# First attention of a three-block kernel: GpSimd takes over the probability multiplies of row tiles 1 to 3

## The chip, the cores and the metric

The kernel runs on one core of a Trainium2 chip. It is one program on five engines with separate instruction queues: TensorE (PE; its weight loads are listed as PEld), VectorE (DVE), ScalarE (ACT), GpSimd (POOL) and SyncE (SP), which wait for each other on semaphores. The metric is the device time of one execution in microseconds.

## The reference, cut to what matters

The whole computation is a transformer block with sparse and sliding-window attention on 512 tokens, followed by two more mixer blocks. The change is in the attention of the first block. For each of 16 heads (two groups of four for each kind of attention) and each query row:

```python
# kind 1: selected blocks (all causal keys here), kind 0: compressed + windowed keys
s = q @ k.T * scale - slope * dist            # NEG_INF where masked
p = softmax(s)                                # exp(s - max) / sum
o = gc[..., 0:1] * o_c + gc[..., 1:2] * o_s + gc[..., 2:3] * o_w   # gates per row and head
# sliding window of 128 with a sink
m = max(max(s), sink);  e = exp(s - m)
prob = e / (sum(e) + exp(sink - m));  o = prob @ v
```

Because a gate is one number per row and head, the kernel multiplies the exponentials by reciprocal sum and gate before the product with the values.

## The kernel before, in words

The attention of the first block works on "quads": four heads of one group g (0 or 1), one row tile t (0 to 3, 128 query rows each) and one kind. Quad number n is 6t + 2·kind + g, so there are 24. In kinds 0 and 1 the scores are 128·(t+1) keys wide (kind 0 also has a compressed part of 32 columns, finished earlier); kind 2, the sliding window, is 128 wide for t = 0 and 256 wide after that. Each quad goes through five steps:

1. TensorE computes the scores of each head into one of four PSUM banks (`pe_slot_scores`, L902 and L903). A "slot" is one bank's worth: two heads at width 256, one at 384 and 512. A slot waits for the exponentials of the slot four before it (`b_exped`).
2. VectorE adds the distances and takes the row minimum (`dve_slot_least`, L2552).
3. ScalarE exponentiates into the SBUF tile `p1` and sums the rows into `st1` (`act_slot_exp`, L1754).
4. VectorE takes the reciprocals of the sums (L2570) and multiplies each head's probabilities in place, four instructions per quad (`dve_quad_scale`: L2579 by reciprocal and gate, L2577 by the reciprocal alone for kind 2). The last one raises `b_scaled`.
5. TensorE waits for `b_scaled`, transposes the quad 128 columns at a time (`pe_quad_turn`, L924; the compressed part, L920, doesn't wait), ScalarE copies the result out of PSUM (L1768), and TensorE multiplies by the values (L948, L945). ScalarE and VectorE then split the output into two parts (L1796, L2593).

The order of the work is written out by hand. On TensorE, `pe_quads` issues for each quad its transposes chunk by chunk, and behind each chunk up to two score slots of later quads, then pairs of value products. On VectorE, `dve_quads` issues for each quad n the minima of the slots that lie four slots ahead, then the multiplies of quad n+1, then outputs that are ready:

```python
    for q in qs:
        for slot in slots_behind(qs, q.n):
            dve_slot_least(k, dve, qs, slot)
        if q.n + 1 < len(qs):
            dve_quad_scale(k, dve, qs, qs[q.n + 1])
```

ScalarE's order is: copy of chunk i of the transposes, then exponentials of the two slots whose scores were issued behind chunk i-1.

GpSimd's work in the whole program is to split the weights, as SyncE loads them, into a high and a low part (L497, L499). Before the attention it splits the output projection's weights; the next ones, of the feed-forward layer (`w_first_hi`), wait for the last attention output (`o_lo`).

Of the kernel before, what the change touches and what calls it, by code (L numbers as in the profile page):

```python
# [9 lines left out]
ALU = mybir.AluOpType  # L10
# [13 lines left out]
GROUPS, PER_G = 2, 4  # L24
# [15 lines left out]
SLOTS_P = 8  # L40
# [22 lines left out]
class Signal:  # L63
# [37 lines left out]

    "gcol gates_ps gates_th gates blocks k_hi k_lo v_copied q_hi q_lo cmp_ps hid_sq hid_a hid_th hid ck_ps ck_hi ck_lo "
    "zeroed sink_neg cmp_scored cmp_least cmp_exped cmp_ready "
    "b_scored b_least b_aux b_exped b_sunk b_scaled b_turned b_pt b_valued o_hi o_lo "

    "scored least exped normed turned pt valued gated "

# [25 lines left out]
class Kernel:  # L133
    def __init__(self, nc, ins, outs, known):
        self.nc, self.ins, self.outs = nc, ins, outs
        self.sig = {n: Signal(nc, n, known) for n in SIGNALS}
        self.x_dram = nc.dram_tensor("x_scratch", [P, TX, D], F32).ap()
        self.gate_dram = nc.dram_tensor("gate_scratch", [3, D], F32).ap()
        self.lay_memory()
        self.list_weights()  # L140
        self.bank_order = bank_order()
        self.ahead = iter(OUT0_AHEAD)
        self.turn8_read = {4: ("turn_tmp", ("h8", TA - 1, 1)), 7: None}
        self.at_before = [None, None]
        sp_program(self, nc.sync)
        pool_program(self, nc.gpsimd)
        pe_program(self, nc.tensor)
        act_program(self, nc.scalar)
        dve_program(self, nc.vector)
# [269 lines left out]
def product_behind(tile):  # L419

    what = tile[0]
    if what == "kv":
        return ("kv", 0, 3) if tile[1] == 0 else ("v", TX - 1)
    if what in ("q", "ff"):
        return (*tile, 3)
    if what in ("o", "gate", "out1"):
        return (what, TX - 1, tile[1])
    if what == "out0":
        return (what, TA - 1, tile[1])
    if what == "down":  # L430
        return (*tile, TX - 1)
    if what == "head":
        return ("z", tile[1], 1)
    if what == "q8":
        return ("row8", 2 * tile[1] + 1, TX - 1)
    return ("kv8", TX + 1) if what == "kv8" else ("z8", 4 * tile[1] + 3)
# [6 lines left out]
def pool_zero_keys(k, pool):  # L443

    s = k.sig
    pool.memset(k.small[:, 3:4], 0.0).then_inc(*s["pool_step"].up())
    pool.wait_ge(*s["pool_step"].now())
    zero = k.small[:, 3:4].rearrange("p (a n) -> p a n", a=1)
    for g in range(GROUPS):
        pool.tensor_copy(k.klo[HD:P, g, 0:2, :], zero[HD:P].to_broadcast([HD, 2, S])).then_inc(*s["pool_step"].up())  # L450
        pool.wait_ge(*s["pool_step"].now())
        pool.tensor_copy(k.klo[0:HD, g, 2:3, :], zero[0:HD].to_broadcast([HD, 1, S])).then_inc(*s["pool_step"].up("k_zero"))
        pool.wait_ge(*s["pool_step"].now())


def pool_program(k, pool):
    s = k.sig
    pool.memset(k.ones[:, :], 1.0).then_inc(*s["ones_set"].up("ones"))
    pool.wait_ge(*s["rms"].at(("x1", 1)))
    for t in range(2, TX):  # L460
        pool.tensor_scalar(k.rows1[:, t, :], k.rows1[:, t, :], k.stat[:, 1, t:t + 1], None, ALU.mult).then_inc(*s["scaled"].up(("x1", t)))
    pair = 0
    for i, (tile, pieces, row0, chunks) in enumerate(k.weights):
        if i == 2:
            pool_zero_keys(k, pool)
        width = max(c0 + n for c0, n, _ in pieces)
        for q in range(0, chunks, 2):
            r = pair % 2
            raw = k.w_raw[:, r, :, 0:width]
            hi, lo = (x[:, q:q + 2, 0:width] for x in k.place(tile))  # L470
            pool.wait_ge(*s[f"w_loaded{r}"].at(pair))
            if q == 0:
                if tile == ("ff", 0):

                    pool.wait_ge(*s["o_lo"].at((TX - 1, 2)))
                elif tile == ("kv8",):

                    pool.wait_ge(*s["y_lo"].at(7))
                elif k.before_in_slot[tile] is not None:
                    pool.wait_ge(*s["prod"].at(product_behind(k.before_in_slot[tile])))  # L480

                if tile == ("ff", 1):
                    pool.wait_ge(*s["rms"].at(("y1", "x", TX - 1)))
                if tile == ("gate", 1):
                    pool.wait_ge(*s["y_added"].at(TX - 1))
                if tile == ("head", 1):
                    pool.wait_ge(*s["rms"].at(("x4", TX - 1)))
                if tile == ("q8", 0):
                    pool.wait_ge(*s["rms"].at(("y3", "x", TA - 1)))
                if tile == ("z8", 0):  # L490
                    pool.wait_ge(*s["rms"].at(("q8", 0)))
            if tile == BY_SCALAR:
                pool.wait_ge(*s["act_step"].at(("w_hi", q)))

            for e in range(2):
                if tile != BY_SCALAR:
                    pool.tensor_scalar(hi[:, e, :], raw[:, e, :], 1.0, 0.0, ALU.mult, ALU.add).then_inc(*s["pool_step"].up())  # L497
                    pool.wait_ge(*s["pool_step"].now())
                m = pool.tensor_tensor(lo[:, e, :], raw[:, e, :], hi[:, e, :], ALU.subtract)  # L499
            m.then_inc(*s["w_split"].up(pair))  # L500
            if q == 0:
                s["w_split"].seen[tile] = s["w_split"].n
            pair += 1
# [73 lines left out]
def quads():  # L577

    out, first = [], 0
    for t in range(TX):  # L580
        for kind in range(3):
            for g in range(GROUPS):
                out.append(Quad(len(out), g, t, kind, first))
                first = out[-1].slots[-1] + 1
    return out
# [12 lines left out]
def turn_number(qs, n, i):  # L598
    return sum(len(q.chunks) for q in qs[:n]) + i


VALUES_AT_ONCE = 2


def value_steps(qs):

    steps, held, step = {}, [], 0
    for q in qs:
        for i in range(len(q.chunks)):
            if len(held) >= VALUES_AT_ONCE:  # L610
                steps[step], held = held[:VALUES_AT_ONCE], held[VALUES_AT_ONCE:]
            if q.g == 1:
# [294 lines left out]
def pe_quad_turn(k, pe, qs, q, i):  # L907

    s, n = k.sig, turn_number(qs, q.n, i)
    what, c = q.chunks[i]  # L910
    if i == 0 and what == "cmp":
        pe.wait_ge(*s["cmp_ready"].at(q.g))
    if what == "keys":
        pe.wait_ge(*s["b_scaled"].at(q.n))
    if n >= 2:
        pe.wait_ge(*s["b_pt"].at(n - 2))
    for e in range(PER_G):
        if what == "cmp":
            x = k.pc[:, q.g, (q.t * PER_G + e) * CMP_W:(q.t * PER_G + e + 1) * CMP_W]
            m = pe.transpose(k.ps[0:CMP_W, 4 + n % 2, e * P:(e + 1) * P], x, k.ident[:, :])  # L920
        else:
            slot, c0 = q.place(e)
            c0 += (c - q.k0) * P
            m = pe.transpose(k.ps[:, 4 + n % 2, e * P:(e + 1) * P], k.p1[:, slot % SLOTS_P, c0:c0 + P], k.ident[:, :])  # L924
    m.then_inc(*s["b_turned"].up((q.n, i)))
# [1633 lines left out]
def dve_quad_scale(k, dve, qs, q):  # L2559

    s, step = k.sig, k.sig["dve_step"]
    f = k.st1[:, q.n % 8, :, :]
    dve.wait_ge(*s["b_exped"].at(q.slots[-1]))
    total = f[:, 1, :]
    if q.kind == 2:
        dve.wait_ge(*s["b_sunk"].at(q.n))
        dve.tensor_tensor(f[:, 2, :], f[:, 1, :], f[:, 3, :], ALU.add).then_inc(*step.up())
        dve.wait_ge(*step.now())
        total = f[:, 2, :]
    dve.reciprocal(f[:, 3, :], total).then_inc(*step.up())  # L2570
    dve.wait_ge(*step.now())
    for e in range(PER_G):
        slot, c0 = q.place(e)
        p = k.p1[:, slot % SLOTS_P, c0:c0 + q.w]
        c = (q.g * PER_G + e) * 3 + 1 + q.kind
        if q.kind == 2:
            m = dve.tensor_scalar(p, p, f[:, 3, e:e + 1], None, ALU.mult)  # L2577
        else:
            m = dve.tensor_scalar(p, p, f[:, 3, e:e + 1], k.gates[:, q.t, c:c + 1], ALU.mult, ALU.mult)  # L2579
    m.then_inc(*s["b_scaled"].up(q.n))  # L2580
# [713 lines left out]
```

## Time and profile before

| | us |
|---|---|
| median of 3 runs (lowest to highest) | 1631.01 (1626.81 to 1631.86) |
| the profiled execution, its own time | 1629.0 |
| its span | 1627.7 |
| PE busy | 1505.7 (93%) |
| DVE busy | 1126.9 (69%) |
| ACT busy | 616.4 (38%) |
| POOL busy | 712.0 (44%) |
| chain that ended last | PE 65%, DVE 16%, ACT 8%, POOL 5% |

The chain that ended last is followed back from the final instruction, so its shares say which engine's work set the end. Over the whole program that is mostly TensorE. The attention of the first block lies between about 146 and 287 us; there the page shows the lowest shares of PE outside the program's start. A queue's instructions run in order, so an instruction that waits holds up everything behind it on its engine.

### The profile page before, as it was taken

The numbers are of one execution on the slowest core, as the hardware profiler recorded it, in microseconds if no ns is written. First come the engines' busy times: TensorE is split into PE (matmuls) and PEld (weight loads), VectorE is DVE, ScalarE is ACT, GpSimd is POOL, SyncE is SP. The second block draws the span as 40 slices with busy tenths as digits, with TensorE's granted clock in tenths as the row PEclk, the third lists the DMA queues.
The fourth block names the chain that finished last, engine by engine and source line by source line (L and its number), as shares of the span: only waits on it lengthen the run. The fifth ranks groups of instructions, "written<-read, shape, count | busy, mean of one in ns | idle before, by whom it ended". The sixth has DMA issues, their size and how long they took to land.

```text
span 1627.7 us, 22505 instructions
## 1 busy us (share of the span) xinstructions
PE 1505.7 (93%) x8093; PEld 1291.1 (79%) x8093; DVE 1126.9 (69%) x2372; ACT 616.4 (38%) x1536; POOL 712.0 (44%) x668
## 2 busy tenths in 40 slices
PE   5998777999999999999999999999997999999997
PEld 4787455788888787877798899889885787899886
DVE  7746566457767769638867677767777588777764
ACT  3324556231221220113544554454455355344431
POOL 6855000347867748685444034303435114524430
PEclk8997799999999999999999999999999999999999
DMA  6622000424434336553311011101102321111121
GB/s 185 198 88 91 1 1 1 143 89 146 142 121 138 118 107 227 184 185 114 124 53 40 14 53 53 33 20 52 53 27 78 121 99 52 58 47 40 65 91 52
DMA packets 115887, 142.61 MB, mean 88 GB/s; under 512 B 11048, under 2 KB 75200, under 8 KB 115776
## 3 DMA queue, kind: packets, MB, share of 16 engines
q1 hardware_dynamic: 89968, 91.77, 18.2%
q10 hardware_dynamic: 25808, 49.40, 9.1%
q8 instruction: 65, 1.06, 0.3%
q14 instruction: 46, 0.38, 0.1%
HBM read 132.74 MB, written 8.40 MB: 87 GB/s over the span
## 4 chain that ended last, share of the span: by engine, by line
PE 65%; DVE 16%; ACT 8%; POOL 5%; issue 4%; DMA 1%; ACTq 0%; SPq 0%; DVEq 0%; POOLq 0%
PE ps L510 17%; PE ps L512 17%; PE ps L511 17%; POOL w_lo L499 3%; PE ps L1486 2%; PE ps L1290 2%; ACT p L2130 2%; POOL w_hi L497 2%; DVE st L2911 2%; PE ps L924 1%; PE ps L982 1%; PE ps L948 1%; DVE p L2579 1%; PE ps L1500 1%; PE ps L902 1%
## 5 line engine op out<-in xcount | busy, mean ns | idle before, releaser
L497 POOL TENSOR_SCALAR w_hi<-w_raw 128x512 fp32r<-128x512 f32 x308 | 236.5, 768 | 640.5 <-PE ps L512 484.9
L499 POOL TENSOR_TENSOR w_lo<-w_raw,w_hi 128x512 fp32r<-128x512 f32 x316 | 443.8, 1405 | 29.8 <-ACT w_hi L1676 4.1
L510 PE MATMUL ps<-w_hi,h_hi 128*128 128x384 f32 (+2 forms) x768 | 278.0, 362 | 8.1 <-POOL w_lo L499 2.9
L512 PE MATMUL ps<-w_hi,h_lo 128*128 128x384 f32 (+2 forms) x768 | 265.6, 346 | 0.0
L511 PE MATMUL ps<-w_lo,h_hi 128*128 128x384 f32 (+2 forms) x768 | 265.0, 345 | 0.0
L510 PE MATMUL ps<-h_hi,w_hi 128*128 128x512 f32 (+1 forms) x616 | 243.9, 396 | 6.3 <-DVE h_lo L2405 2.6
L512 PE MATMUL ps<-h_hi,w_lo 128*128 128x512 f32 (+1 forms) x616 | 236.7, 384 | 0.0
L511 PE MATMUL ps<-h_lo,w_hi 128*128 128x512 f32 (+1 forms) x616 | 236.5, 384 | 0.0
L2629 DVE SCALAR_TENSOR_TENSOR mod_acc<-mod_piece,csil,mod_acc 128x512 f32<-128x512 f32 x140 | 158.6, 1172 | 19.8 <-DMA mod_piece<-in_ada_w 16.0
L510 PEld LDWEIGHTS ps<-w_hi,h_hi 128*128 128x128 f32 x768 | 147.2, 192 | 20.4 <-POOL w_lo L499 4.3
L511 PEld LDWEIGHTS ps<-w_lo,h_hi 128*128 128x128 f32 x768 | 147.4, 192 | 8.3 <-issue 0.5
L512 PEld LDWEIGHTS ps<-w_hi,h_lo 128*128 128x128 f32 x768 | 146.4, 191 | 9.1
L510 PEld LDWEIGHTS ps<-h_hi,w_hi 128*128 128x128 f32 x616 | 118.1, 192 | 27.7 <-POOL w_lo L499 3.3
L512 PEld LDWEIGHTS ps<-h_hi,w_lo 128*128 128x128 f32 x616 | 117.8, 191 | 23.2
L511 PEld LDWEIGHTS ps<-h_lo,w_hi 128*128 128x128 f32 x616 | 118.3, 192 | 19.7
L2130 ACT ACTIVATE p<-ps,st 128x768 f32<-128x768 f32 (+1 forms) x96 | 72.8, 759 | 117.7 <-DVE st L2911 117.7
L510 PE MATMUL ps<-w_hi,g_hi 128*128 128x512 f32 x240 | 96.0, 400 | 5.1 <-POOL w_lo L499 4.7
L2911 DVE TENSOR_REDUCE st<-ps 128x1 f32<-128x768 f32 (+1 forms) x96 | 73.7, 774 | 37.8 <-PE ps L1290 37.8
L512 PE MATMUL ps<-w_hi,g_lo 128*128 128x512 f32 x240 | 94.3, 393 | 0.0
L511 PE MATMUL ps<-w_lo,g_hi 128*128 128x512 f32 x240 | 94.1, 392 | 0.0
L2141 ACT ACTIVATE p_turned_hi<-ps 128x512 fp32r<-128x512 f32 (+1 forms) x80 | 37.6, 469 | 80.1 <-PE ps L1306 79.9
L1290 PE MATMUL ps<-k_hi,q 128*128 128x384 f32 (+1 forms) x160 | 46.6, 356 | 19.8 <-ACT p L2130 19.8
(337 smaller groups left out, 2999.4 us busy)
## 6 DMA issues: line engine op xcount, KB each, us to landing
mod_piece<-in_ada_w ACTq DMA_DIRECT2D x96, 256.0 KB, 3.0
w_raw<-in_w_gate_up SPq DMA_DIRECT2D x88, 256.0 KB, 3.1
w_raw<-in_a_w_in SPq DMA_DIRECT2D x128, 128.0 KB, 2.2
w_raw<-in_w_down SPq DMA_DIRECT2D x22, 512.0 KB, 4.5
w_raw<-in_b_w_in SPq DMA_DIRECT2D x20, 512.0 KB, 3.6
w_raw<-in_w_out SPq DMA_DIRECT2D x16, 512.0 KB, 3.9
w_raw<-in_w_in SPq DMA_DIRECT2D x8, 512.0 KB, 4.1
w_raw<-in_w_o SPq DMA_DIRECT2D x8, 512.0 KB, 3.9
```

The lines of the kernel that those rows point to most:

```text
L497: pool.tensor_scalar(hi[:, e, :], raw[:, e, :], 1.0, 0.0, ALU.mult, ALU.add).then_inc(*s["pool_step"].up())
L499: m = pool.tensor_tensor(lo[:, e, :], raw[:, e, :], hi[:, e, :], ALU.subtract)
L510: pe.matmul(out, a[0], b[0], start=start, stop=False)
L511: pe.matmul(out, a[0], b[1], start=False, stop=False)
L512: return pe.matmul(out, a[1], b[0], start=False, stop=stop)
L902: pe.matmul(out, x, k.khh[:, q.g, q.kind, keys], start=True, stop=False)
L1290: m = pe.matmul(k.ps[:, bank, 0:cols], k.q6[:, b, sub, t * P:(t + 1) * P], kk[:, b, sub, k0 + j * cols:k0 + (j + 1) * cols], start=first, ...
L1486: m = pe.matmul(k.ps[:, b, 0:384], k.q8[x][:, pair % 2, e, t * P:(t + 1) * P], k.k8[kk][:, pair // 2, b * 384:(b + 1) * 384], start=i == 0 ...
L2130: act.activation(folded(k.p6[:, i % 2 if sub == 0 else 2, 0:w], bs), bank_view(k, bs, P, cols), ACT.Exp, bias=f[:, sub:sub + 1], scale=-1. ...
L2141: act.activation(k.at6[:, chunks[0]:chunks[-1] + 1, (t % 2) * P:(t % 2 + 1) * P], turned6(k, j)[:, 0:P * len(chunks)].rearrange("p (c n) - ...
L2629: m = dve.scalar_tensor_tensor(acc, piece, w, acc, ALU.mult, ALU.add)
L2911: dve.tensor_reduce(k.st6[:, i % 4, sub:sub + 1], bank_view(k, bs, P, cols), AX.XY if len(bs) == 2 else AX.X, ALU.min).then_inc(*s["head_l ...
```

## The change

For quads with t ≥ 1 (`POOL_SCALES_FROM = 1`), VectorE stops after the reciprocals and raises `b_total`; GpSimd waits for it, does the four multiplies and raises `b_scaled_p`, for which TensorE's transposes now wait. GpSimd does this for the 18 quads between the last split of the output projection's weights and the first split of the feed-forward weights.

```diff
+def pool_quad_scale(k, pool, q):
+
+    s, f = k.sig, k.st1[:, q.n % 8, :, :]
+    pool.wait_ge(*s["b_total"].at(q.n))
+    for e in range(PER_G):
+        slot, c0 = q.place(e)
+        p = k.p1[:, slot % SLOTS_P, c0:c0 + q.w]
+        c = (q.g * PER_G + e) * 3 + 1 + q.kind
+        if q.kind == 2:
+            m = pool.tensor_scalar(p, p, f[:, 3, e:e + 1], None, ALU.mult)
+        else:
+            m = pool.tensor_scalar(p, p, f[:, 3, e:e + 1], k.gates[:, q.t, c:c + 1], ALU.mult, ALU.mult)
+    m.then_inc(*s["b_scaled_p"].up(q.n))
...
                 if tile == ("ff", 0):
+                    for quad in quads():
+                        if quad.t >= POOL_SCALES_FROM:
+                            pool_quad_scale(k, pool, quad)
...
+POOL_SCALES_FROM = 1
...
     if what == "keys":
-        pe.wait_ge(*s["b_scaled"].at(q.n))
+        pe.wait_ge(*s["b_scaled_p" if q.t >= POOL_SCALES_FROM else "b_scaled"].at(q.n))
...
         total = f[:, 2, :]
+    if q.t >= POOL_SCALES_FROM:
+        dve.reciprocal(f[:, 3, :], total).then_inc(*s["b_total"].up(q.n))
+        return
     dve.reciprocal(f[:, 3, :], total).then_inc(*step.up())
     dve.wait_ge(*step.now())
```

VectorE at quad 13 (row tile 2, kind 0, group 1), before: `st_93` is the tile of sums and reciprocals, `p_95` the probabilities, `ISA` the minimum of one head and its read-out.

```order
L2570 RECIPROCAL st_93<-st_93 128x4 [waits b_exped]
L2579 TENSOR_SCALAR p_95<-p_95,st_93,gates 128x384 [waits dve_step]
L2579 TENSOR_SCALAR p_95<-p_95,st_93,gates 128x384 x3
L2593 TENSOR_TENSOR h_lo<-ps,h_hi 128x4x128 [waits o_hi]
L2552 ISA ps,st_93<-ps,dist 128x384 [waits b_scored]
L2552 ISA st_93 128x1
```

The same place after the change (line numbers are 19 to 22 higher there):

```order
L2590 RECIPROCAL st_93<-st_93 128x4 [waits b_exped]
L2615 TENSOR_TENSOR h_lo<-ps,h_hi 128x4x128 [waits o_hi]
L2571 ISA ps,st_93<-ps,dist 128x384 [waits b_scored]
L2571 ISA st_93 128x1
L2571 ISA ps,st_93<-ps,dist 128x384 [waits b_scored]
```

The four multiplies are gone from VectorE's queue, and the next quad's minima stand directly behind the reciprocal and the output.

GpSimd between the last split for the output projection and the first for the feed-forward layer, before:

```order
L497 TENSOR_SCALAR w_hi<-w_raw 128x512
L499 TENSOR_TENSOR w_lo<-w_raw,w_hi 128x512 [waits pool_step]
L497 TENSOR_SCALAR w_first_hi<-w_raw 128x512 [waits o_lo,w_loaded0]
L499 TENSOR_TENSOR w_first_lo<-w_raw,w_first_hi 128x512 [waits pool_step]
```

and after, the first quads and the last rows of the 18:

```order
L517 TENSOR_TENSOR w_lo<-w_raw,w_hi 128x512 [waits pool_step]
L467 TENSOR_SCALAR p_95<-p_95,st_93,gates 128x256 [waits b_total,w_loaded0]
L467 TENSOR_SCALAR p_95<-p_95,st_93,gates 128x256 x3
...
L467 TENSOR_SCALAR p_95<-p_95,st_93,gates 128x512 x3
L465 TENSOR_SCALAR p_95<-p_95,st_93 128x256 [waits b_total]
L465 TENSOR_SCALAR p_95<-p_95,st_93 128x256 x3
...
L515 TENSOR_SCALAR w_first_hi<-w_raw 128x512 [waits o_lo]
```

72 instructions, in 18 groups of four with one wait each, have moved in ahead of the wait for `o_lo`.

## Rows read from the trace of the kernel before

**Rows 1.** Waits, 180 to 290 us: waiter, awaited: total us, times, longest.
```profile
POOL w_first_hi L497 <- DVE h_lo L2593: 131.9, 1, 131.9
...
PEld ps L924 <- DVE p L2579: 18.5, 8, 4.4
...
PE ps L924 <- DVE p L2579: 14.6, 6, 4.2
```

**Rows 2.** Chain that ended last, shares by line, 185 to 287.4 us.
```profile
by line: PE ps L924 18.3%; PE ps L948 13.5%; ACT p L1754 11.6%; DVE p L2579 11.3%; PE ps L902 8.2%; PE ps L903 8.1%; issue 7.4%; DVE ps L2552 5.7%; DVE p L2577 4.5%; PE ps L945 3.0%; DVE st L2570 1.8%; PE ps L920 1.4%; ACT pt_late L1768 1.1
```

**Rows 3.** Timeline: start us, duration us, engine, line, operation, count [idle before].
```profile
213.88 0.18 DVE L2570 RECIPROCAL st<-st 128x4 f32<-128x4 f32 x1 [1.88 <-ACT p L1754]
214.09 1.65 DVE L2579 TENSOR_SCALAR p<-p,st,gates 128x384 f32<-128x384 f32 x4
...
215.79 0.66 PE L924 MATMUL ps<-ident,p 128*128 128x128 f32 x4 [1.65 <-DVE p L2579]
...
221.56 0.18 DVE L2570 RECIPROCAL st<-st 128x4 f32<-128x4 f32 x1 [3.14 <-ACT p L1754]
```

**Rows 4.** Timeline of VectorE: four multiplies of a quad, other widths.
```profile
185.29 1.38 DVE L2579 TENSOR_SCALAR p<-p,st,gates 128x256 f32<-128x256 f32 x4
...
198.47 1.14 DVE L2577 TENSOR_SCALAR p<-p,st 128x256 f32<-128x256 f32 x4
...
247.27 1.92 DVE L2579 TENSOR_SCALAR p<-p,st,gates 128x512 f32<-128x512 f32 x4
```

**Rows 5.** Three GpSimd lines: count, durations min/median/max ns, first and last start.
```profile
L461 POOL TENSOR_SCALAR rows<-rows,stat x2: 2842/3123/3404, 14.2 to 17.6; 128x1024 f32<-128x1024 f32 x2
...
L450 POOL CAST k_lo<-small x2: 1038/1042/1045, 56.2 to 58.0; 64x1024 fp32r<-64x1024 f32 x2
...
L452 POOL CAST k_lo<-small x2: 612/614/616, 57.3 to 59.1; 64x512 fp32r<-64x512 f32 x2
```

**Rows 6.** Timeline near 14 us: GpSimd's scaling of rows, VectorE beside it.
```profile
14.16 0.75 DVE L2434 TENSOR_SCALAR rows<-rows,stat 128x1024 f32<-128x1024 f32 x1
14.23 6.24 POOL L461 TENSOR_SCALAR rows<-rows,stat 128x1024 f32<-128x1024 f32 x2 [13.41 <-DVE stat L2381]
```

**Rows 7.** Quad 6: VectorE's multiplies, and TensorE's first transposes of them.
```profile
176.96 1.39 DVE L2579 TENSOR_SCALAR p<-p,st,gates 128x256 f32<-128x256 f32 x4
...
181.05 1.09 PE L924 MATMUL ps<-ident,p 128*128 128x128 f32 x8
```

**Rows 8.** The same pair of rows for quads 19 and 22.
```profile
254.49 1.92 DVE L2579 TENSOR_SCALAR p<-p,st,gates 128x512 f32<-128x512 f32 x4
...
257.25 1.05 PE L924 MATMUL ps<-ident,p 128*128 128x128 f32 x4
...
279.07 1.14 DVE L2577 TENSOR_SCALAR p<-p,st 128x256 f32<-128x256 f32 x4
...
281.65 0.66 PE L924 MATMUL ps<-ident,p 128*128 128x128 f32 x4
```

**Rows 9.** Timeline: a VectorE result that GpSimd waits for.
```profile
288.17 0.69 DVE L2593 TENSOR_TENSOR h_lo<-ps,h_hi 128x512 fp32r<-128x512 f32 x1 [1.02 <-ACT h_hi L1796]
...
289.03 0.62 POOL L497 TENSOR_SCALAR w_first_hi<-w_raw 128x512 fp32r<-128x512 f32 x1 [131.94 <-DVE h_lo L2593]
```

**Rows 10.** Busy us (x instructions) by engine, then granted clock, DMA share, GB/s.
```profile
185.00:287.00 102.00, 78.14 (x420) 50.29 (x420) 63.03 (x213) 63.98 (x184) 0.00 (x0) 0.92 0.00 1
165.00:175.00 10.00, 5.78 (x25) 4.34 (x22) 3.88 (x20) 3.21 (x10) 0.00 (x0) 0.50 0.00 0
227.00:231.00 4.00, 0.40 (x4) 0.40 (x5) 2.28 (x6) 1.66 (x6) 0.00 (x0) 1.00 0.00 0
231.00:235.00 4.00, 4.00 (x23) 3.95 (x21) 2.41 (x11) 1.73 (x5) 0.00 (x0) 0.57 0.00 0
```

**Rows 11.** The chain of waits: one 512-wide score matmul at either clock.
```profile
250.13 0.23 PE ps L903
...
256.17 0.43 PE ps L903
```

More of the change, by code:

```diff
@@ L103 @@
     "zeroed sink_neg cmp_scored cmp_least cmp_exped cmp_ready "
-    "b_scored b_least b_aux b_exped b_sunk b_scaled b_turned b_pt b_valued o_hi o_lo "
+    "b_scored b_least b_aux b_exped b_sunk b_total b_scaled b_scaled_p b_turned b_pt b_valued o_hi o_lo "
     "scored least exped normed turned pt valued gated "
```

## The prediction

> **What bounds the kernel here.** Only the first attention changes, so I read its stretch alone. The waits of that stretch come first [rows 1]: TensorE and its weight loads stood idle 14.6 and 18.5 us for VectorE's gated multiply (L2579), before the transposes of L924. GpSimd stood idle 131.9 us in one piece: it is free for the whole attention. The chain that ended last [rows 2] shows where 185 to 287.4 us went: VectorE's multiplies L2579 and L2577 hold 11.3% + 4.5% of 102.4 us, about 16 us; the rest is transposes, scores, exponentials, values. The reader is to see that no engine is full there: in 185 to 287 us TensorE is busy 78 of 102 us (with modelled ends), VectorE 63, ScalarE 64 [rows 10]. A loop of waits bounds the stretch. The timeline of one turn shows it [rows 3]: the reciprocal of quad 13 at 213.88 waits for ScalarE's exponentials, the four multiplies run 214.09 to 215.74, TensorE starts the transposes at 215.79, 0.05 us later, and the next quad's reciprocal comes at 221.56, again after exponentials. From tile 2 on a quad of kinds 0 and 1 fills all four score banks, and half or all of the next quad's scores stand in TensorE's queue behind the transposes that wait for the multiplies. VectorE can't use the time that it gets back: what is next in its queue is the minimum of scores that TensorE has not issued yet. So the length of the multiplies is paid whole, whichever engine does them, and the question is what they last on GpSimd.
>
> **What goes.** VectorE loses 72 instructions in 18 groups of four. A group lasts 1.38 us (256 wide, gated), 1.14 (256, kind 2), 1.92 (512) [rows 4] and 1.65 (384) [rows 3].
>
> **What comes, and its price.** No row shows GpSimd multiplying by a scalar read per partition at these widths. The nearest is L461, which has all the same marks: float32 in place, in SBUF, times a column of another tile. It took 2842 and 3404 ns at 1024 columns [rows 5]. The longer one had VectorE's 0.75 us row scaling beside it [rows 6]; the difference is 0.56 us. I take 2842, because after the change VectorE has no tensor_scalar in this stretch. The Trainium skill (SBUF — State Buffer, Who interferes with whom) says that GpSimd and a VectorE operation in a 2-port mode hold one pair of ports exclusively, and that an operation with at most one SBUF input outside such a mode doesn't contend; the pair of durations agrees with that rule, and if instead the 3404 ns held throughout, the sum would be some 12 us higher.
>
> For the part that doesn't grow with width I use GpSimd's casts: 1042 ns at 1024 columns against 614 at 512 [rows 5] give 0.836 ns a column and 186 ns fixed. L461 then is 186 ns + 2.594 ns a column, and one multiply is 850, 1182 and 1514 ns at 256, 384 and 512, a group of four 3.40, 4.73 and 6.06 us. Bounds: all of L461 proportional to width gives groups of 2.84, 4.26 and 5.68 us; the casts' rate gives 1.60, 2.03 and 2.46 us (their slope alone, fixed parts hidden behind one another, 0.86, 1.28 and 1.71, below VectorE's: a gain); and if all that L461 has over a cast, 1.8 us, were fixed per instruction, a group would be some 8.8 to 9.7 us. I go by L461, the row of the same form.
>
> Sum over the quads (number = 6 x tile + 2 x kind + group):
> - Quads 8 and 9: 2 x (3.40 - 1.38) = 4.0 us.
> - The six of kind 2 (10, 11, 16, 17, 22, 23): 6 x (3.40 - 1.14) = 13.6.
> - 12 to 15: 4 x (4.73 - 1.65) = 12.3.
> - 18 to 21: 4 x (6.06 - 1.92) = 16.6.
> - 6 and 7: about 0. The multiplies of quad 6 end at 178.35, but TensorE, busy with values at the slow clock, transposes them only at 181.05 [rows 7]: 2.7 us of cover against 2.0 more. In quad 7 the two score slots stand behind the compressed transposes, which don't wait, so its extra time lies beside VectorE's minima.
>
> Together 46.5 us. The wider kind 0 quads (12, 13, 18, 19) also have two slots of scores ahead of the wait, so VectorE can do two minima meanwhile; I give nothing for it, because ScalarE's queue holds their exponentials behind the copy of the first waiting transpose.
>
> Cover elsewhere: quad 19's multiplies end at 256.41 and are read at 257.25, quad 22's end at 280.21 and are read at 281.65 [rows 8], 0.8 and 1.4 us; minus 2.2. I found nothing like it for the others.
>
> The handover: VectorE to itself costs 0.03 us (reciprocal ends 214.06, multiply starts 214.09 [rows 3]), VectorE to GpSimd 0.17 (288.86 to 289.03 [rows 9]); 16 x 0.14 = 2.2 us. GpSimd's end to TensorE I take as equal.
>
> The clock: the mean granted clock of 185 to 287 us is 0.92 [rows 10], with only the two levels 1.2 and 2.4 GHz that is 16% of the time at 1.2. A drop follows an idle TensorE: 0.40 us busy in 227 to 231, then 0.57 in 231 to 235. In 165 to 175 us, with TensorE busy little more than half, it stayed at 1.2 GHz throughout. A 512-wide score step on the chain lasts 0.43 us at the low level and 0.23 at the high one [rows 11]. After the change TensorE idles 2 to 4 us longer in nearly every quad, so nearly each begins at 1.2 GHz. TensorE's lines hold 52.5% of the chain [rows 2], 54 us; if all of it ran low, it would cost some 34 us more; if no dip is added, 0. Thirteen more dips like the five or so of now, each 3.5 us long with half of that on the chain, cost 13 x 0.8 = 10 us, and some will last longer: I take 15.
>
> Total: 46.5 - 2.2 + 2.2 + 15 = 61.5 us on the profiled execution's 1629.0 gives 1690.5. The median of the runs, 1631.0, is 2.0 above that execution: 1692.5. Everything behind the attention shifts whole, since the feed-forward weights waited for the last output before [rows 1] and still do; GpSimd has nothing queued behind its multiplies that could start sooner.
>
> **Rivals.**
> - GpSimd is near VectorE's speed. It decides where a 384 group takes under about 1.5 us, VectorE's 1.65 less the handover; the place is the same wait of TensorE at L924. For it: GpSimd's L497, two operations with constants, does 512 columns in 0.62 us [rows 9], and the casts are as fast. Against it: L461. Slope alone gives (0.86-1.38)x2 + (0.86-1.14)x6 + (1.28-1.65)x4 + (1.71-1.92)x4 = -5.0 us, with the handover -2.8; with the fixed parts +6.9 - 2.2 + 2.2 = +6.9. The middle is +2: 1633 us, not slower than can be told. The Trainium skill (GPSIMD Engine Reference, Engine selection) says that one-input elementwise work on GpSimd is roughly line-rate; by that rule this rival would hold, and the trace agrees for constants only.
> - The second scalar costs as much as the first. L461 has one, the gated quads two. One costs (2842 - 1042)/1024 = 1.76 ns a column over a cast; again that for quads 8, 9, 12 to 15 and 18 to 21 is 4 x 1.76 x (256x2 + 384x4 + 512x4) = 29 us, and some 3 for 6 and 7, whose cover is then used up: 1692.5 + 32 = 1724 us. For it nothing but the count; against it, that L497's second operation shows no such price.
> - The per-partition scalar costs a fixed 1.8 us each time: groups of 9 us, 16 x about 7.5 = 120 us and the clock, about 1765 us. Two rows of one width can't exclude it.
> - The clock stays low for the whole stretch: 19 us over the forecast, 1711; inside its own range.
>
> **How the numbers follow.** Forecast 0.68, its own range 1670 (proportional widths, -8, and no clock cost, -15) to 1712 (low clock throughout); near VectorE's speed 0.12; second scalar 0.15; fixed price 0.05. The 80% range leaves out the fast rival and the fixed price: 1660 to 1725. A measurement of this kernel can tell about 0.3%, 4.9 us. The fast rival is split 0.03 faster, 0.06 no change, 0.03 slower; all else is slower: 0.03, 0.06, 0.91.
>
> **What would show it.** L467 and L465 on GpSimd: means near 850, 1180, 1510 ns; two-scalar and one-scalar forms at 256 equal (if L467 is longer, the second rival). TensorE's idle at L924 put down to GpSimd, 70 us or more against 33 for L2579 now. The granted clock of the stretch at 0.6 to 0.8 instead of 0.92, and the stretch 60 us longer, with the rest of the span unchanged. I am wrong if the multiplies last under 0.5 us at 512, if VectorE's minima run while GpSimd multiplies in most quads, or if the time turns up behind the attention.

## The result, and the profile after

The changed kernel takes 1656.76 us (median of 4 runs, 1653.25 to 1659.2) against 1629.55 us of the kernel before (median of 4): a ratio of 1.0167, 95% interval 1.015 to 1.0184, 27 us slower. A second set of runs gave 1655.99 against 1629.46, 1.0161 (1.0139 to 1.0183). The forecast was slower, 1692.5 us; the direction is right, the size more than twice too large, and the time lies below the stated range.

Where TensorE waits in the attention, rows of the waits from 180 to 330 us (waiter, awaited: total us, times, longest), against [rows 1]:

```profile
POOL p L467 <- DVE st L2590: 74.7, 12, 19.0
...
PEld ps L943 <- POOL p L467: 26.5, 8, 5.6
...
PE ps L943 <- POOL p L467: 22.7, 8, 5.4
...
PEld ps L943 <- POOL p L465: 16.9, 6, 4.6
PE ps L943 <- POOL p L465: 14.1, 6, 4.4
```

Before, for kind 2, from 180 to 290 us:

```profile
PE ps L924 <- DVE p L2577: 3.2, 4, 1.8
```

TensorE's idle time ahead of its transposes was 14.6 + 3.2 us for VectorE's multiplies; now it is 22.7 + 14.1 us for GpSimd's. The chain by line over the same part of the program (quad 8's reciprocal to the last output), against [rows 2]:

```profile
by line: PE ps L943 17.4%; POOL p L467 16.3%; POOL p L465 13.7%; ACT p L1773 10.0%; PE ps L967 9.6%; issue 7.5%; PE ps L921 6.6%; PE ps L922 6.6%; DVE ps L2571 4.2%; PE ps L964 3.0%; DVE st L2590 1.8%; ACT pt_late L1787 0.9%; DVE st L2571 0
```

The multiplies now hold 16.3% + 13.7% of 132.5 us of the chain, 40 us where they held 16. So some 24 of the 29 us by which this stretch is longer in the profile stand in the multiplies themselves.

What one multiply lasts on GpSimd, the groups of instructions by shape (busy us, mean ns, idle before), against [rows 4 and 5]:

```profile
L465 POOL TENSOR_SCALAR p<-p,st 128x256 f32<-128x256 f32 x24 | 21.7, 923 | 24.9 <-DVE st L2590 24.9
...
L467 POOL TENSOR_SCALAR p<-p,st,gates 128x512 f32<-128x512 f32 x16 | 12.1, 769 | 23.6 <-DVE st L2590 23.6
...
L467 POOL TENSOR_SCALAR p<-p,st,gates 128x384 f32<-128x384 f32 x16 | 10.3, 662 | 24.4 <-DVE st L2590 24.4
...
L467 POOL TENSOR_SCALAR p<-p,st,gates 128x256 f32<-128x256 f32 x16 | 8.7, 556 | 26.7 <-DVE st L2590 26.7
```

These are the rows that decide. The form with one scalar and one operation lasts 923 ns at 256 columns, near the 850 that the forecast had. The gated form, with two scalars and two operations, lasts only 556, 662 and 769 ns at 256, 384 and 512 columns, where the forecast had 850, 1182 and 1514.

The timeline of quad 13 and its successor, against [rows 3]:

```profile
223.45 0.18 DVE L2590 RECIPROCAL st<-st 128x4 f32<-128x4 f32 x1 [1.88 <-ACT p L1773]
...
223.73 2.59 POOL L467 TENSOR_SCALAR p<-p,st,gates 128x384 f32<-128x384 f32 x4 [4.39 <-DVE st L2590]
224.12 0.56 DVE L2571 CUSTOM_DVE_ANT_0 ps<-ps,dist 128x384 f32<-128x384 f32 x1
...
226.37 1.07 PE L943 MATMUL ps<-ident,p 128*128 128x128 f32 x4 [2.65 <-POOL p L467]
...
227.96 0.59 ACT L1773 ACTIVATE p<-ps,st 128x384 f32<-128x384 f32 x1
...
233.70 0.18 DVE L2590 RECIPROCAL st<-st 128x4 f32<-128x4 f32 x1 [4.32 <-ACT p L1773]
```

The loop has kept its shape. GpSimd's four multiplies run from 223.73 to 226.32, TensorE's transposes follow 0.05 us later, and the next reciprocal comes at 233.70, 7.4 us behind the end of the multiplies (5.8 before). VectorE does start a minimum at 224.12, beside GpSimd, but ScalarE takes up the exponential of that slot only at 227.96, behind the copy of the first transposes: the time that VectorE got back isn't passed on. Of the 16 quads from 8 on, minima run beside GpSimd's multiplies in four only (12, 13, 18 and 19, the wide ones of kind 0), as the prediction had it.

Two more places, quads 8 and then 22 and 23:

```profile
187.94 0.17 DVE L2590 RECIPROCAL st<-st 128x4 f32<-128x4 f32 x1
...
188.21 2.16 POOL L467 TENSOR_SCALAR p<-p,st,gates 128x256 f32<-128x256 f32 x4 [2.90 <-DVE st L2590]
...
306.44 3.62 POOL L465 TENSOR_SCALAR p<-p,st 128x256 f32<-128x256 f32 x4 [7.01 <-DVE st L2590]
...
310.11 1.09 PE L943 MATMUL ps<-ident,p 128*128 128x128 f32 x8 [0.43 <-POOL p L465]
...
310.51 3.62 POOL L465 TENSOR_SCALAR p<-p,st 128x256 f32<-128x256 f32 x4 [0.45 <-DVE st L2590]
```

The handover from VectorE to GpSimd takes 0.10 us (188.11 to 188.21). Quad 22's transposes begin at 310.11, 0.05 us behind its multiplies, where they began 1.4 us behind them before [rows 8]: TensorE had other work until shortly before, and of 2.5 us of longer multiplying it sat idle for 0.43 (1.10 in the profile of e9, the same kernel).

The busy times of that stretch, then granted clock, before and after (against [rows 10]):

```profile
185.08:288.17 103.09, 79.31 (x423) 50.94 (x424) 63.10 (x213) 64.50 (x185) 0.00 (x0) 0.92 0.00 1
```

```profile
187.94:320.36 132.42, 91.63 (x423) 57.31 (x424) 39.89 (x150) 64.79 (x185) 48.45 (x64) 0.81 0.00 1
```

It lasts 132.4 us instead of 103.1 (129.2 in the profile of e9). The mean granted clock fell from 0.92 to 0.81, so the time at the low level of 1.2 GHz rose from 16 to 50 us (41 in e9's).

### The profile page after: what moved, and what is told of

Its sections match the earlier page's. It is cut to its first block, busy times and chain, and to the rows that moved or that the text cites. A ratio compares the mean times of both kernels' runs of the same rounds, so it can differ in the third digit from the quotient of the medians.

```text
span 1657.9 us, 22505 instructions
## 1 busy us (share of the span) xinstructions
PE 1515.6 (91%) x8093; PEld 1295.2 (78%) x8093; DVE 1100.5 (66%) x2300; ACT 616.9 (37%) x1536; POOL 763.2 (46%) x740
## 3 DMA queue, kind: packets, MB, share of 16 engines
q1 hardware_dynamic: 89968, 91.77, 18.1%
## 4 chain that ended last, share of the span: by engine, by line
PE 64%; DVE 15%; ACT 8%; POOL 7%; issue 4%; DMA 1%; ACTq 0%; SPq 0%; DVEq 0%; POOLq 0%
PE ps L528 17%; PE ps L530 16%; PE ps L529 16%; POOL w_lo L517 3%; PE ps L1505 2%; PE ps L943 2%; PE ps L1309 2%; ACT p L2149 2%; POOL w_hi L515 2%; DVE st L2933 2%; POOL p L467 1%; PE ps L1001 1%; POOL p L465 1%; PE ps L967 1%; PE ps L1519 1%
## 5 line engine op out<-in xcount | busy, mean ns | idle before, releaser
L2651 DVE SCALAR_TENSOR_TENSOR mod_acc<-mod_piece,csil,mod_acc 128x512 f32<-128x512 f32 x140 | 157.1, 1161 | 18.8 <-DMA mod_piece<-in_ada_w 14.9
L943 PE MATMUL ps<-ident,p 128*128 128x128 f32 x216 | 41.0, 331 | 47.6 <-POOL p L467 22.7
L943 PEld LDWEIGHTS ps<-ident,p 128*128 128x128 f32 x216 | 29.9, 168 | 65.8 <-POOL p L467 26.5
```

The lines of the kernel that those rows point to most:

```text
L2651: m = dve.scalar_tensor_tensor(acc, piece, w, acc, ALU.mult, ALU.add)
```

## The experiments

**e1: a second operation for kind 2.** Each ratio below is to the kernel before, with its 95% interval.

```diff
         if q.kind == 2:
-            m = pool.tensor_scalar(p, p, f[:, 3, e:e + 1], None, ALU.mult)
+            m = pool.tensor_scalar(p, p, f[:, 3, e:e + 1], 1.0, ALU.mult, ALU.mult)
```

> The changed kernel, with one edit: the multiply of kind 2 on GpSimd (L465) gets a second operation, a multiplication by the constant 1.0; results are the same. Theory 1 (the number of operations in the instruction sets GpSimd's rate: one is slow, two are fast): L465 falls from 923 ns to the 549 ns of the gated form at 256 columns, a group of four from 3.62 to 2.16 us, six groups save 8.8 us, all on the loop: about 1648 us. Rival (kind 2 is slow because of its place or of what VectorE does beside it): 923 ns stays and the time stays near 1657. Rival (a tensor scalar in the second place is needed for the fast form): 923 ns stays.

Measured: 1641.29 us, ratio 1.007 (1.0047 to 1.0094), below the 1648 expected. The multiply fell from 923 to 479 ns:

```profile
L465 POOL TENSOR_SCALAR p<-p,st 128x256 f32<-128x256 f32 x24 | 11.0, 479 | 26.1 <-DVE st L2590 26.1
```

One more operation on the same data halves the instruction. The operation and its constant come together in one edit; no run tells them apart. The form is even 77 ns shorter than the gated one, so a second scalar read per partition costs some 80 ns, an estimate (662 and 769 ns lie as far above a line through 479 ns here and the 1112 ns at 1024 columns of e4). Both rivals fall. The kernel gained 15.5 us though, where 10.7 us of multiplying went away, so I ran it again.

**e10 and e9: the same once more, beside the changed kernel.**

> e1 once more (kind 2 on GpSimd with a second operation, 479 ns instead of 923, so 10.5 us less multiplying on the six groups). Theory (lengths are paid one to one, low clock at 0.2 us a us): 10.5 us and 2 to 3 us for the clock, 12 to 14 us below the run beside it. Rival (the 15.5 us of the first comparison are real and something else goes with the short form): 15 us or more.

> The changed kernel once more, beside the next run, since four runs of each leave the distance between them uncertain by some 5 us. Theory: 1656 to 1658.

Measured: e10 1639.99 us, ratio 1.0061 (1.004 to 1.0082); e9 1655.99. The distance is 16.0 us again, in the range of the rival, where I had expected 12 to 14. What goes with the short form is in part the clock. From quad 8's reciprocal to the last output e9 takes 129.2 us in its profile and e10 115.5, 13.7 less: 10.7 of multiplying and 3.0 more. These 3.0 us lie for the most part in two of the turns from one reciprocal to the next, that of quad 11 to 12 and that of 13 to 14, first in e9:

```profile
206.88:215.88 9.00, 5.05 (x18) 3.39 (x20) 1.43 (x6) 3.62 (x11) 3.62 (x4) 0.64 0.00 0
222.86:233.09 10.23, 7.58 (x34) 3.17 (x32) 3.05 (x11) 4.34 (x13) 2.59 (x4) 0.83 0.00 0
```

then in e10:

```profile
204.73:210.48 5.75, 3.59 (x20) 2.00 (x20) 1.32 (x6) 3.63 (x11) 1.84 (x4) 1.00 0.00 0
217.46:226.15 8.69, 6.04 (x34) 2.77 (x32) 2.94 (x11) 4.35 (x13) 2.59 (x4) 1.00 0.00 0
```

The first turn is 3.25 us shorter, 1.78 by the multiplies and 1.5 more; the second has the same multiplies and is 1.5 us shorter. In both the granted clock is 1.00 instead of 0.64 and 0.83, so 6.5 and 3.5 us at the low level cost 1.5 us each, 0.23 and 0.44 us a us. The first pair of profiles shows the same: these turns take 5.77 and 8.68 us in e1's, 8.99 and 10.25 in the changed kernel's. The other 2.3 of the 16.0 us lie outside this stretch or between the runs, about as wide as the intervals, and their cause stays open.

**e2: the gate left out, so that all 72 multiplies have the one-operation form.** The kernel leaves out a factor of the result; only its time is of use.

```diff
         else:
-            m = pool.tensor_scalar(p, p, f[:, 3, e:e + 1], k.gates[:, q.t, c:c + 1], ALU.mult, ALU.mult)
+            m = pool.tensor_scalar(p, p, f[:, 3, e:e + 1], None, ALU.mult)
```

> The changed kernel, with the gates left out of the multiplies of kinds 0 and 1 on GpSimd, so that all 72 instructions have one scalar and one operation. Theory 1: they last 0.92, 1.24 and 1.56 us at 256, 384 and 512 columns (2.5 ns a column and 283 ns, from the 923 ns of L465 and the 2842 ns of L461), groups of 3.62, 4.9 and 6.2 us, and the kernel is 25 to 27 us slower than the changed one: about 1683. If the recorded forecast's other terms (clock 15 us) were right once the multiplies are as long as forecast, 1692. Rival (a column costs what the gated form shows, 0.88 ns, and only a fixed part differs): 0.92, 1.03, 1.15 us and about 1668.

Measured: 1683.03 us, ratio 1.0321 (1.0298 to 1.0345).

```profile
L467 POOL TENSOR_SCALAR p<-p,st 128x512 f32<-128x512 f32 x16 | 24.7, 1564 | 22.4 <-DVE st L2590 22.4
...
L467 POOL TENSOR_SCALAR p<-p,st 128x384 f32<-128x384 f32 x16 | 19.6, 1245 | 24.9 <-DVE st L2590 24.9
...
L467 POOL TENSOR_SCALAR p<-p,st 128x256 f32<-128x256 f32 x16 | 14.5, 928 | 23.4 <-DVE st L2590 23.4
```

928, 1245 and 1564 ns: 2.5 ns a column. The first theory holds to a few ns and to the microsecond. This is about the kernel that the forecast had priced, and it takes 1683 us, not 1692. Its multiplies are even 3 us longer in sum than forecast (49.5 us more than before, not 46.5), so the other terms of the sum, the clock's 15 us above all, are some 12 us too high: 52.4 us slower against 49.5 - 2.2 + 2.2 + 15.

**e3: VectorE multiplies twice.** The kernel before, with

```diff
     m = dve.tensor_scalar(... four heads, as before ...)
+    if q.t >= 1:
+        m.then_inc(*step.up()); dve.wait_ge(*step.now())
+        for e in range(PER_G):
+            m = dve.tensor_scalar(p, p, 1.0, None, ALU.mult)
     m.then_inc(*s["b_scaled"].up(q.n))
```

> The kernel before, where VectorE multiplies each quad of row tiles 1 to 3 once more, by the constant 1.0, before it signals; GpSimd takes no part. Theory (the loop pays for the length of the multiplies, whoever does them): 23.9 us more on quads 8 to 23, less some 2 us of cover, plus a few us of slower TensorE clock: 1653 to 1657, near the changed kernel. Rival (the change costs its time through the handover between engines or through GpSimd's queue): VectorE has slack and the time stays under 1645.

Measured: 1653.47 us, ratio 1.0141 (1.0119 to 1.0164), 22.8 us slower, with GpSimd out of it. The second pass is shorter than the first:

```profile
216.13 1.65 DVE L2579 TENSOR_SCALAR p<-p,st,gates 128x384 f32<-128x384 f32 x4
217.81 1.17 DVE L2586 TENSOR_SCALAR p<-p 128x384 f32<-128x384 f32 x4
```

From start to end a group is 0.93, 1.20 and 1.46 us longer at the three widths, 18.1 us over quads 8 to 23, not the 23.9 that I had expected. That the time still fell into the range is in part luck: I had summed 5.8 us too much of multiplying, and the clock, by an estimate 4 to 5 us for some 20 us more at the low level (at 0.22 us each, below), made up for most of it. So the loop pays for length on VectorE as it does on GpSimd, and the handover isn't what costs. The stretch from quad 8's reciprocal to the last output in the profiles of these kernels. "Multiplies" is the growth of the groups of quads 8 to 23, "rest" what is then left, and the last column the time at the low clock; the rows of e1, e3 and e2 follow the table:

| kernel | stretch, us | longer by | of it multiplies | rest | at 1.2 GHz, us |
|---|---|---|---|---|---|
| before | 103.1 | | | | 16 |
| e1 | 115.4 | 12.3 | 13.9 | -1.6 | 23 |
| e3 | 122.5 | 19.4 | 18.1 | 1.3 | 34 |
| e9, the changed kernel | 129.2 | 26.1 | 24.6 | 1.5 | 41 |
| changed kernel | 132.4 | 29.3 | 24.6 | 4.7 | 50 |
| e2 | 155.5 | 52.4 | 49.5 | 2.9 | 56 |

```profile
187.81:303.21 115.40, 80.32 (x423) 51.73 (x424) 39.42 (x149) 64.46 (x185) 37.78 (x64) 0.90 0.00 1
```

```profile
188.80:311.26 122.46, 86.10 (x423) 54.10 (x424) 80.30 (x277) 64.60 (x185) 0.00 (x0) 0.86 0.00 1
```

```profile
189.58:345.09 155.51, 90.67 (x423) 59.40 (x424) 40.13 (x149) 65.30 (x185) 73.31 (x64) 0.82 0.00 1
```

The column of multiplies is for the changed kernel 2 x 0.78 + 6 x 2.48 + 4 x 0.94 + 4 x 1.10. The rest is between -2 and 5 us, and holds cover, handover and clock.

**e5 and e6: TensorE kept busy while it waits.** Six (in the changed kernel) or four (in the kernel before) matmuls ahead of the wait, into the bank that the transposes overwrite. The wait for that bank (`b_pt`), which stood behind the one for the multiplies, moves ahead of the matmuls:

```diff
+    if what == "keys" and i == (q.kind == 0) and q.t >= 1:
+        for _ in range(6):
+            pe.matmul(k.ps[:, 4 + n % 2, :], k.qst[:, q.head0, q.t * P:(q.t + 1) * P], k.khh[:, q.g, 0, :], start=True, stop=True)
     if what == "keys":
         pe.wait_ge(...)
```

> The changed kernel, where TensorE does six more 512-wide score matmuls into the bank that the next transposes overwrite, ahead of its wait for the multiplies of each quad from quad 6 on (1.4 us each time at the high clock, in an idle time of 2 to 5 us). The result is unchanged. Theory (each us at the low clock costs the loop about 0.2 us, from the four kernels so far): the granted clock of the attention rises from 0.81 towards 0.9 or more, and the kernel gets 4 to 8 us faster than the changed one: 1649 to 1653. The recorded forecast's clock term (15 us) would give 1642. Rival (the clock costs nothing, the rest is order and cover): the clock rises and the time stays at 1657, or gets worse by what the added matmuls delay.

Measured: 1656.34 us, ratio 1.0162 (1.0142 to 1.0183): as without them. The profiled execution, the fastest of the four at 1651.3, shows the clock at 0.96 and the stretch 8.5 us shorter than the changed kernel's:

```profile
188.72:312.59 123.87, 101.46 (x525) 65.42 (x526) 39.30 (x150) 64.71 (x185) 48.41 (x64) 0.96 0.00 1
```

Against e9's profile it is 5.3 us shorter. The clock was higher in the other runs too: the four spent 103 us on average at the low level, where those of the changed kernel spent 123 and 128. But the median didn't move. Either the clock gave back nothing, or the added matmuls took it again by delaying what stands behind them; this pair doesn't tell which.

> The kernel before, with four such matmuls ahead of the wait of each quad from quad 6 on (0.9 us at the high clock). Theory: the low clock's share of the attention, 16 us of 103, falls and 0 to 3 us are gained: 1628 to 1631. Rival: where TensorE has no idle time (quads 6, 19, 22) the matmuls delay it by 0.9 us each and more at the low clock, and the kernel is 1 to 5 us slower.

Measured: 1637.44 us, ratio 1.0049 (1.0031 to 1.0066), 8.6 us slower, more than the rival expected. Shorter waits leave less idle time to fill and as much to delay, which would explain it but isn't shown. These two don't price the clock. The runs themselves give an average: each comes with its granted clock, so with its time at the low level, 2 x (1 - clock) x time. Within one kernel that varies from run to run, and over all 123 runs, each taken against the mean of its kernel in its set, one us more at the low level goes with 0.22 us more time (standard error 0.02, correlation 0.67). That is how the two go together in the whole program, not an edit of the clock alone; the two turns above, 0.23 and 0.44, show that the price depends on the place. The changed kernel's runs have 125 us at the low level on average (two sets, 127.6 and 123.4), those of before 103: 22 us more, by that average 5 us of time.

**e7: three heads on VectorE, the fourth on GpSimd by two operations.**

```diff
-    for e in range(PER_G):            # GpSimd, and kind 2 with a second operation as in e1
+    for e in range(3, PER_G):
...
+        pe.wait_ge(*s["b_scaled"].at(q.n))
+        if q.t >= POOL_SCALES_FROM:
+            pe.wait_ge(*s["b_scaled_p"].at(q.n))
```

> From quad 6 on VectorE multiplies three heads of a quad and GpSimd the fourth, by an instruction with two operations (0.48 to 0.77 us), and TensorE waits for both. Theory 1 (they run side by side): each group is 0.35 to 0.48 us shorter than VectorE's four, 6 us over 16 quads: 1625. Theory 2 (VectorE's multiply and GpSimd's hold the same pair of ports exclusively, as the Trainium skill, SBUF — State Buffer, Who interferes with whom, says, and as the 2.73 us of the four multiplies of quad 0 beside GpSimd's splits suggest): they run one after another, a group lasts VectorE's three and GpSimd's one, 1.5 to 2.2 us, and the kernel is as fast as before or up to 4 us slower, 1630 to 1634.

Measured: 1627.65 us, ratio 0.9989 (0.9978 to 1.0001): no difference that can be told. Quad 12 in the timeline:

```profile
209.11 0.18 DVE L2592 RECIPROCAL st<-st 128x4 f32<-128x4 f32 x1 [1.41 <-ACT p L1775]
...
209.33 1.53 DVE L2604 TENSOR_SCALAR p<-p,st,gates 128x384 f32<-128x384 f32 x3
209.40 0.86 POOL L467 TENSOR_SCALAR p<-p,st,gates 128x384 f32<-128x384 f32 x1 [4.33 <-DVE st L2592]
...
210.91 0.66 PE L945 MATMUL ps<-ident,p 128*128 128x128 f32 x4 [0.47 <-DVE p L2604]
```

VectorE's three multiplies take 1.53 us, where three quarters of 1.65 are 1.24, and GpSimd's one 0.86 instead of 0.66. They are in each other's way. The Trainium skill's rule on the shared pair of ports (SBUF — State Buffer, Who interferes with whom), by which one of them is held off for a whole instruction, gives the direction, but not the size: the group isn't as long as the two one after another, 1.90 us, and the measurement decides. Neither theory is right as written. VectorE's three last 1.22, 1.53 and 1.83 us for the gated quads at 256, 384 and 512 columns and 1.10 us for kind 2, where its four lasted 1.38, 1.65, 1.92 and 1.14. Over the 16 quads that is 1.4 us less, not 6: three quarters of the gain are lost.

**e4: the second operation in the row scaling at the start.**

```diff
-        pool.tensor_scalar(k.rows1[:, t, :], k.rows1[:, t, :], k.stat[:, 1, t:t + 1], None, ALU.mult)
+        pool.tensor_scalar(k.rows1[:, t, :], k.rows1[:, t, :], k.stat[:, 1, t:t + 1], 1.0, ALU.mult, ALU.mult)
```

> The kernel before, with one edit far from the attention: the row scaling on GpSimd at the start (L461) gets a second operation, a multiplication by 1.0. Theory 1: its two instructions fall from 3.40 and 2.84 us to 1.2 to 1.8 us (0.88 ns a column and 325 ns, from the gated form), TensorE's 2.8 us of waits for it shrink, and GpSimd starts the first weights some 4 us sooner: 1 to 4 us faster than before, 1626 to 1628. Rival (in-place work at 1024 columns is slow in any form): no change.

Measured: 1623.78 us, ratio 0.9966 (0.9949 to 0.9983), more than expected. The very instruction from which the forecast took its price, against [rows 5]:

```profile
L461 POOL TENSOR_SCALAR rows<-rows,stat x2: 1112/1394/1675, 14.0 to 15.7; 128x1024 f32<-128x1024 f32 x2
```

2842 ns have become 1112, with the same tiles, the same width and the same scalar. TensorE's first weight product starts at 24.08 instead of 25.07. More of the gain lies ahead of the attention: its first quad's reciprocal starts at 149.7 and 150.8 us in the two profiles with this edit (e4, e8), and at 150.8 to 155.7 in the ten without it, median 154.2; the profile before is the earliest of the ten. So some 4 us of the gain of 6.9 are there by the medians, though one profile of a kernel says little. The clock of the first 50 us doesn't explain it: it was 0.97 with the edit, and 1.00 in most profiles without it. Where the rest comes from isn't shown.

**e8: e4 and e7 together.**

> The kernel before with the row scaling of e4 (a second operation on GpSimd's L461) and the split of e7 (VectorE three heads, GpSimd the fourth with two operations). Theory (the two gains lie in different stretches and add up: 5 to 7 us at the start, 0 to 3 us in the attention): 1621 to 1624. Rival (the split's small gain was noise, or is given back): as e4, 1624 to 1625.

Measured: 1622.55 us, ratio 0.9959 (0.9944 to 0.9975). It beats the kernel before and the changed one; from e4 alone it can't be told.

## Why the prediction was wrong

**What bounds the attention: right.** The loop of waits pays for the length of the multiplies: 24.6 us of longer groups and 27 us in the time; 18.1 and 23 for e3, without GpSimd; 49.5 and 52 for e2. VectorE starts minima beside GpSimd in four of the 16 quads, and their exponentials wait behind ScalarE's copy (224.12 and 227.96 in the timeline); in the other twelve it starts none.

**The price of a multiply: the step that failed.** The prediction took L461 as "the row of the same form" because it shared in-place work, float32 and a scalar read per partition. It shared these with all the multiplies, but its number of operations only with kind 2. For the six quads of kind 2 the forecast term was 13.6 us and measured 14.9, in part by luck: the prediction didn't know that the number of operations mattered. For the ten gated quads from 8 on it was 32.9 us (4.0 + 12.3 + 16.6), and measured 9.7: 23 of the 34 us by which the forecast was too high. e1 and e4 show the cause: with the data and the scalar kept, a second operation takes 923 to 479 ns and 2842 to 1112 ns. The evidence stood in [rows 9]: L497, two operations, 0.62 us at 512 columns. The prediction set it aside as "constants only"; it compared rows that differed in two things, and credited the wrong one. The rival of the second scalar was half right: it has a price, but by the estimate above 80 ns fixed, not 1.76 ns a column.

**The rival near VectorE's speed** had the gated form nearly right (0.83 ns a column between 256 and 512 here, 0.84 for its casts) and kind 2 wrong. The truth lay between two cases that I had held apart for all 72 instructions at once. The Trainium skill's line that one-input work is roughly line-rate on GpSimd (GPSIMD Engine Reference, Engine selection) agrees with the traces for the form with two operations (0.83 ns a column, as the casts), not for the one with one (2.5 ns).

**The clock: the right sign, sized too high.** 15 us forecast; 22 us more at the low level at 0.22 us each, 5 us, by the runs. The price per dip (0.8 us of 3.5) agrees with that average. The amount doesn't: thirteen dips of 3.5 us are 45 us at the low level, and the step from 10 to 15 us had no row behind it. With the multiplies shorter than forecast the low time grew by 22 us over the runs (25 and 34 in the stretches of the two profiles); e2, with the multiplies about as forecast, shows 40 us more in its stretch and a rest of only 2.9 us.

**Cover and handover: small, as said.** Handover 0.07 us more a quad, 1.1 us in all, forecast 0.14 and 2.2. Quad 22's cover was seen in TensorE's idle time (0.43 us for 2.5 us of longer multiplying). With the four terms as measured (gated 9.7, kind 2 14.9, clock 5, handover 1.1) and the cover as forecast the sum is 28.5 us, and 27 were measured.

**A sign that didn't tell.** TensorE's idle time for GpSimd, matmuls and weight loads added, was to be 70 us or more, and is 80 (22.7 + 26.5 + 14.1 + 16.9), with less than half of the forecast slowdown. The sum counts the same wait twice, once for each kind of instruction, and its 33 us of before left out kind 2. The sign on the two forms asked only whether L467 would be longer; it came out shorter.

**Behind the attention** little moved. In the two profiles the last output is 32.2 us later; 2.9 us of that were there at quad 8's reciprocal already, and 2 us were given back behind the last output. Both are within what profiles differ by without a cause in the change: the attention's first reciprocal spreads over 4.9 us in ten profiles with one code ahead of it, and the part behind the last output differs by 3.4 us between e1 and e10, one kernel.

## What to carry to other kernels

When an operation's price is taken from another line, list what the two instructions differ in, the number of operations included, and look for a second row that differs in just one of these; if the changed kernel holds two forms, price each by itself. On GpSimd, a scaling by one scalar per partition is worth a second, idle operation. And where a loop of waits bounds a stretch, moving its work to an idle engine gains nothing unless that engine does it in less time, handover included.

## What the runs showed of the hardware that was not expected

- GpSimd's tensor_scalar with one operation: 923 ns at 256 columns, 1245 at 384, 1564 at 512, 2842 at 1024. With a second one: 479 at 256, 1112 at 1024. A second scalar per partition: some 80 ns more, an estimate.
- VectorE's three tensor_scalar and GpSimd's one beside each other, at 384 columns: 1.53 us instead of 1.24, and 0.86 instead of 0.66.
- One us more at the low TensorE clock goes with 0.22 us more time in this kernel, over 123 runs, and cost 0.23 and 0.44 us in two turns of the loop; filling TensorE's waits with matmuls raised the granted clock of the attention from 0.81 and 0.84 to 0.96 in the profiles and gained nothing in the median.
